# Expert tiles fixed per expert, overflow tiles between them, routing begun during attention, and results scattered by token

## The chip, the cores and the metric

The kernel runs on one core of a Trainium2 chip. Its engines are TensorE (matrix products; PE in the rows, and PEld for its weight loads), VectorE (DVE), ScalarE (ACT), GpSimd (POOL) and SyncE (SP), which here only issues DMAs. They run side by side and order themselves by semaphores. The metric is the time of one execution on the device in microseconds (us), lower is better.

## The reference

One layer of an encoder for 1024 tokens of width 1024, in float32. A first half (norm, one projection, a gated delta rule with 4 heads, a sliding window attention with 8 heads, an output projection) gives `x`; the change leaves its arithmetic alone. The second half is a mixture of experts:

```python
gl = tok @ w_group + b_group                     # 4 groups
p_top, g_idx = lax.top_k(jax.nn.softmax(gl), 1)  # the best group
el_sel = ...                                     # logits of the 4 experts in that group
e_val, e_idx = lax.top_k(el_sel, TOP_K)          # the best 2 of the 4
e_w = jax.nn.softmax(e_val, axis=-1) * p_top
...
for e in range(N_EXPERTS):                       # 16 experts, width 256
    gu = tok @ w_gate_up[e]
    act = jax.nn.silu(gu[:, :D_EXPERT]) * gu[:, D_EXPERT:]
    y = y + gates[:, e:e + 1] * (act @ w_down[e])
```

and the output is `x + y`. So there are 2048 picks, two for each token. With the inputs of these runs an expert gets 59 to 232 of them. In tiles of 128 rows that is 9 experts with one tile and 7 with two, 23 tiles.

## The kernel before

**Attention.** `run_tiles` runs over 8 tiles of 128 tokens, written out in full for each engine. A tile's `body` holds the delta rule and the attention; the projections of the next tile and the `late` part of the previous one (output projection, norm, router logits `lg`) are put between its steps. The last tile has no next tile, and its own `late` comes behind it alone. The normed rows go to `h_mid` in HBM and the residual to `x_mid`.

**Routing.** With all logits there, VectorE computes picks and gates for all 8 tiles at once (L1214 to L1237). TensorE sums the picks to ranks within each expert. From ranks and the number of tiles of each expert VectorE computes each pick's slot. One-hot rows (`hot_mod`, `hot_div`, L1268 and L1269) are multiplied on TensorE, which inverts the table: for each slot the token in it (`idx`, L1271).

**Experts.** The slots fill tiles in the order of the experts, an expert's second tile right behind its first, and there are always 31 of them (`SLOT_TILES`), the most that 2048 picks can need. `run_slots` writes the first three and last two steps out and has the rest in a loop. Per tile `m`: GpSimd gathers 128 rows of `h_mid` (L1426); TensorE turns them (L363), multiplies them with gate and up (64 passes of 128x128, L360) and the previous tile's result with `w_down`; VectorE copies the turned rows (L1278) and makes SwiGLU (L1285, L1287); VectorE and ScalarE copy half of the result each (L1294, L889); SP stores it to `y_slots`. TensorE's order in a step is: turn `m + 1`, gate/up `m`, down `m - 1`. Weights, gathered rows and results have two buffers each, and the weights' expert number is read from a table. If tile `m` isn't used (`m >= n_used`), its weights are not loaded and its gate/up and down are a stand-in of 4 columns; it is gathered, turned, copied and stored all the same.

**Combining.** When all tiles are stored, GpSimd gathers for each of 8 token tiles the two result rows of each token (L1434, L1436), VectorE scales them by the gates and adds them to `x` (L1310, L1314), and SP stores.

The whole of the expert stage's order on TensorE is this:

```python
def step(m, b, u):
    if not isinstance(m, int) or m < SLOT_TILES - 1:
        turn_rows(m + 1, 1 - b, u + b)
    gate_up(m, b, u)
    if later(m):
        down(m - 1, 1 - b, u - 1 + b)
```

## Time and profile before

| | us |
|---|---|
| median of 3 runs | 1135.8 |
| lowest and highest | 1134.96 and 1136.03 |
| the profiled execution | 1135.93 |
| its span, first to last instruction | 1134.2 |
| TensorE busy | 996.4 (88%) |
| VectorE busy | 569.7 (50%) |
| ScalarE busy | 237.8 (21%) |
| GpSimd busy | 116.4 (10%) |
| data moved by DMA | 155.38 MB |

The profile is of one execution, times in it are us from the start of the span, and what lies between span and time is 1.7 us. In the timeline a row has its start, its length, engine, line, operation, output and inputs, how many instructions are merged, and in square brackets how long the engine had been idle before it and who ended that. Float32 products go through TensorE in two passes, so a product counts as two there. An indirect DMA's row on GpSimd is the issue alone, not the transfer.

### The profile page before, as it was taken

What the parts mean: (1) busy time and instruction counts of PE and PEld (TensorE: products, weight loads), DVE (VectorE), ACT (ScalarE), POOL (GpSimd) and SP (SyncE); (2) the same over time, 40 slices, a digit from 0 to 9 for tenths busy, and PEclk for the clock granted to TensorE, in tenths of its full rate; (3) what the DMA queues carried; (4) which work ended last, traced back from release to release, by engine and by line L of the source; (5) the groups of instructions that cost most, each with busy time, mean ns of one, the idle gap of its engine ahead of it and who ended that gap; (6) DMA issues with size and microseconds to landing.
All of it is one profiled execution on the core that took longest, in us unless ns stands there. A gap on an engine that the chain in (4) does not pass through costs nothing.

```text
span 1134.2 us, 17951 instructions
## 1 busy us (share of the span) xinstructions
PE 996.4 (88%) x6940; PEld 693.9 (61%) x6940; DVE 569.7 (50%) x1654; ACT 237.8 (21%) x489; POOL 116.4 (10%) x182
## 2 busy tenths in 40 slices
PE   6979999999999999999999787643999999999820
PEld 2446656656656656656656556423888888888620
DVE  1455766765765756766756656345222121212445
ACT  1333233233233233233233221000000000000110
POOL 6020010010010010010010010000100000000124
PEclk9999999999999999999999978775899999999855
DMA  9700100100100100100000001045799999998668
GB/s 324 279 19 1 38 5 35 38 12 28 38 19 21 38 1 38 38 8 30 20 1 38 20 0 39 19 185 212 258 366 365 370 361 372 358 369 327 220 220 351
DMA packets 57312, 155.38 MB, mean 137 GB/s; under 512 B 4240, under 2 KB 5520, under 8 KB 57248
## 3 DMA queue, kind: packets, MB, share of 16 engines
q1 hardware_dynamic: 48752, 129.59, 30.9%
q0 software_dynamic: 6768, 24.64, 6.1%
q8 instruction: 44, 0.72, 0.3%
q10 hardware_dynamic: 1728, 0.26, 0.1%
q14 instruction: 20, 0.16, 0.0%
HBM read 125.65 MB, written 28.84 MB: 136 GB/s over the span
## 4 chain that ended last, share of the span: by engine, by line
PE 84%; DVE 7%; DMA 3%; issue 2%; POOL 2%; ACT 1%; SPq 0%; POOLq 0%; ACTq 0%; DVEq 0%
PE pm L360 77%; PE pm L363 8%; DMA w_sb<-h_mid,w_sb 1%; DMA w_sb<-y_slots,w_sb 1%; DVE X L1107 1%; DMA y_slots<-w_sb 1%; POOL w_sb L1436 1%; DVE w_sb L1200 1%; POOL w_sb L1434 1%; ACT ci L725 0%; DMA xt<-in_x 0%; DVE hT L935 0%; DVE bs L914 0%; DVE bs L913 0%; DVE bs L912 0%
## 5 line engine op out<-in xcount | busy, mean ns | idle before, releaser
L360 PE MATMUL pm<-w_sb,hT 128*128 128x512 f32 (+1 forms) x768 | 314.1, 564 | 2.9 <-DVE hT L935 2.8
L360 PE MATMUL pm<-w_sb 128*128 128x128 f32 (+2 forms) x1688 | 256.4, 314 | 8.6 <-DVE w_sb L1269 8.5
L360 PEld LDWEIGHTS pm<-w_sb,hT 128*128 128x128 f32 x768 | 144.2, 192 | 149.5 <-issue 141.2
L360 PEld LDWEIGHTS pm<-w_sb 128*128 128x128 f32 x1688 | 206.6, 196 | 42.0 <-issue 33.0
L360 PE MATMUL pm<-wo_sb,pT 128*128 128x512 f32 x256 | 120.5, 627 | 1.2 <-ACT pT L782 1.2
L1294 DVE COPY w_sb<-pm 128x512 f32<-128x512 f32 x31 | 21.4, 691 | 175.7 <-PE pm L360 168.3
L977 DVE SCALAR_TENSOR_TENSOR pqkv<-ci,cw,pqkv 128x128 f32<-128x128 f32 x288 | 77.6, 344 | 21.5 <-ACT pqkv L730 21.1
L360 PEld LDWEIGHTS pm<-wo_sb,pT 128*128 128x128 f32 x256 | 50.3, 201 | 60.4 <-issue 58.8
L1278 DVE TENSOR_TENSOR w_sb<-pm,gain 128x512 f32<-128x512 f32 x62 | 39.9, 685 | 40.4 <-PE pm L363 38.9
L1426 POOL DMA_INDIRECT w_sb<-h_mid,w_sb x31 | 29.2, 943 | 289.0 <-PE pm L363 262.7
L1107 DVE TENSOR_TENSOR X<-X,pm 128x256 f32<-128x256 f32 (+1 forms) x40 | 16.8, 419 | 80.2 <-PE pm L360 80.2
L881 ACT ACTIVATE w_sb<-pm 128x256 f32<-128x256 f32 x31 | 11.9, 383 | 213.0 <-PE pm L360 209.9
L1378 POOL TENSOR_TENSOR tail<-tail,rows 128x512 f32<-128x512 f32 x8 | 10.2, 1273 | 404.0 <-ACT aTm L749 404.0
L1023 DVE TENSOR_TENSOR sc<-sc,pm 128x512 f32<-128x512 f32 x16 | 11.0, 688 | 79.7 <-PE pm L360 79.7
L363 PE MATMUL pm<-ident,w_sb 128*128 128x128 f32 x248 | 37.7, 303 | 13.1 <-DMA w_sb<-h_mid,w_sb 11.2
L363 PEld LDWEIGHTS pm<-ident,w_sb 128*128 128x128 f32 x248 | 32.7, 157 | 26.1 <-issue 16.6
L363 PE MATMUL pm<-ident,y_mix 128*128 128x128 f32 x128 | 20.5, 312 | 22.9 <-DVE y_mix L1184 14.1
L889 ACT ACTIVATE w_sb<-pm 128x512 f32<-128x512 f32 x31 | 18.5, 597 | 84.2 <-PE pm L360 75.2
L818 ACT ACTIVATE Y<-pm 128x256 f32<-128x256 f32 (+1 forms) x48 | 18.3, 381 | 81.9 <-PE pm L360 81.9
L363 PEld LDWEIGHTS pm<-ident,y_mix 128*128 128x128 f32 x128 | 16.8, 159 | 27.8 <-DVE y_mix L1184 14.5
L719 ACT ACTIVATE tail<-pm 128x512 f32<-128x512 f32 (+1 forms) x24 | 12.7, 528 | 100.3 <-PE pm L360 100.3
L360 PEld LDWEIGHTS pm<-Y,aTm 64*64 64x64 f32 x576 | 22.1, 135 | 15.4 <-issue 11.8
(238 smaller groups left out, 1228.7 us busy)
## 6 DMA issues: line engine op xcount, KB each, us to landing
w_sb<-in_w_gate_up SPq DMA_DIRECT2D x23, 2048.0 KB
w_sb<-in_w_down SPq DMA_DIRECT2D x23, 1024.0 KB
y_slots<-w_sb SPq DMA_DIRECT2D x31, 512.0 KB
w_sb<-in_w_in SPq DMA_DIRECT2D x5, 2048.0 KB, 17.0
xt<-in_x SPq DMA_DIRECT2D x8, 512.0 KB, 3.5
wo_sb<-in_w_out SPq DMA_DIRECT2D x1, 4096.0 KB, 22.6
sc<-in_x SPq DMA_DIRECT2D x8, 512.0 KB, 3.5
x_mid<-sc SPq DMA_DIRECT2D x8, 512.0 KB, 2.6
```

The costliest lines, as they stand in the source:

```text
L360: return pe.matmul(o_, lhsT=l_, rhs=r_, start=start, stop=stop, skip_group_check=True)
L363: return pe.transpose(o_, in_, ident[:, :])
L719: act.activation(dst, pm[BANK[c]][:, 0:n], ACT.Copy).then_inc(F.chunk_copied, 1)
L818: act.activation(Yd[rows_], heads(pm[3], CH)[rows_], ACT.Copy).then_inc(B.y_copied, 1)
L881: act.activation(tnh, pm[2 + b][:, 0:DE], ACT.Tanh, scale=0.5).then_inc(M.tanh_ready, 1)
L889: act.activation(yo[b][:, 512:], pm[7][:, :], ACT.Copy).then_inc(M.y1_ready, 1)
L977: ins = v.scalar_tensor_tensor(cv[:, i, :], ci[:, i, j:j + P], cw[:, j, i:i + 1], cv[:, i, :], ALU.mult, ALU.add)
L1107: v.tensor_tensor(Xd[rows_], Xd[rows_], heads(pm[2], CH)[rows_], ALU.subtract).then_inc(B.x_updated, 1)
L1200: step(v.tensor_tensor(dst, a, b, op))
L1278: v.tensor_tensor(hgT[b][:, 4 * n:4 * n + 4, :], heads(pm[n]), wide(gain2[:, 4 * n:4 * n + 4]), ALU.mult).then_inc(M.hT_ready, 1)
L1294: v.tensor_copy(yo[b][:, 0:512], pm[6][:, :]).then_inc(M.y0_ready, 1)
L1426: g.indirect_dma_start(hg[m % 2], None, h_mid, bass.IndirectOffsetOnAxis(idx[:, m:m + 1], 0)).then_inc(gathered[m % 2], 16)
```

## The change

- There are again 31 steps, but 16 of them are fixed, one for each expert (`ORDER`, static), and 15 are overflow steps for ranks from 128 on (dynamic), which read their expert from a table. They alternate: S0, S1, D0, S2, D1, S3, ..., D13, S15, D14. With 7 experts over 128 picks, D0 to D6 are full and D7 to D14 are empty. Where the step is empty TensorE now skips the turn too. Row numbers that no token has are out of range, and the DMAs leave such rows out (`bounds_check`).
- All steps are written out. Fixed experts' weights have four buffers (three in the space of `w_in`, one in pieces of attention's tiles), the overflow steps one. The weights of experts 0 to 2 are loaded when the last tile's projections are done.
- The picks of tiles 0 to 5 are routed in the last tile's `body` (`picks_ahead`, `rank_ahead`) and `late` (`rows_ahead`); tiles 6 and 7 afterwards. The table is now by rank and expert, and there is a second one with the gates.
- The two halves of a result are scaled by the gate as they are copied, and GpSimd scatters them by pick to `y_picks`. The end is 16 plain loads, two sums for each tile and 8 stores.

VectorE in the last tile. Before (`upper` is the causal mask, `sc` the residual, `ctmp` and `Y` masks of the delta rule):

```order
L1080 TENSOR_TENSOR ctmp<-ctmp,upper 128x512 [waits dT_exp]
L1023 TENSOR_TENSOR sc<-sc,pm 128x512 [waits out_done,xr_loaded]
L1023 TENSOR_TENSOR sc<-sc,pm 128x512 [waits out_done]
L1084 TENSOR_TENSOR ctmp<-ctmp,bs 128x512
L1086 TENSOR_TENSOR Y<-pm,ctmp 64x4x64 [waits kk_done,back_step]
```

After, with 29 operations of `picks_ahead` in between:

```order
L1316 TENSOR_TENSOR ctmp<-ctmp,upper 128x512 [waits dT_exp]
L1063 TENSOR_REDUCE w_sb<-lg 128x6 [waits route_iotas,back_step]
L1050 TENSOR_TENSOR w_sb<-lg,w_sb 128x6x4 [waits route_route_step]
...
L1124 TENSOR_TENSOR w_sb<-w_sb 128x16 [waits route_route_step] x6
L1258 TENSOR_TENSOR sc<-sc,pm 128x512 [waits out_done,xr_loaded]
L1258 TENSOR_TENSOR sc<-sc,pm 128x512 [waits out_done]
L1322 TENSOR_TENSOR ctmp<-ctmp,bs 128x512
```

The first of them waits for GpSimd's iotas. GpSimd at the end of attention, before:

```order
L1405 TENSOR_TENSOR kn<-kn,bs 128x512 [waits kn_turned,eg_ready,kn_ready]
L1413 IOTA w_sb 128x128 [waits lg_ready]
L1414 CAST w_sb<-w_sb 128x128 [waits pool_made]
L1415 IOTA w_sb 128x8 [waits pool_made]
L1416 CAST w_sb<-w_sb 128x8 [waits pool_made]
```

GpSimd at the same place after the change, and on to the first gathers and scatters (L1651, L1659):

```order
L1628 TENSOR_TENSOR kn<-kn,bs 128x512 [waits kn_turned,eg_ready,kn_ready]
L1636 IOTA w_sb 128x128 [waits chunk_done]
...
L1645 MEMSET w_sb 128x16 [waits pool_made]
L1651 DMA qkvT<-h_mid,w_sb 128x1024 [waits route_rows_ready,mid_stored]
L1651 DMA pqkv<-h_mid,w_sb 128x1024
L1651 DMA qkvT<-h_mid,w_sb 128x1024 [waits slots_turned,route_spill_ready]
L1651 DMA pqkv<-h_mid,w_sb 128x1024 [waits slots_turned]
L1659 DMA y_picks<-tail,w_sb 2048x1024 [waits slots_y1_ready,slots_y0_ready]
L1651 DMA qkvT<-h_mid,w_sb 128x1024 [waits slots_turned]
```

The iotas no longer wait for the last logits, the third gather waits for the overflow rows, and from then on gathers and scatters take turns.

TensorE from the first tile on, before:

```order
L363 MATMUL pm<-ident,w_sb 128x128 x7
L360 MATMUL pm<-w_sb 128x128 [waits w1_loaded0,slots_hT_ready]
L360 MATMUL pm<-w_sb 128x128 x31
L363 MATMUL pm<-ident,w_sb 128x128 [waits slots_hT_ready,gathered0]
L363 MATMUL pm<-ident,w_sb 128x128 x7
L360 MATMUL pm<-w_sb 128x128 [waits w1_loaded1,slots_hT_ready]
```

After (`qkvT` and `pqkv` are now the buffers of gathered rows):

```order
L427 MATMUL pm<-ident,qkvT 128x128 [waits route_table_ready,gathered0]
L427 MATMUL pm<-ident,qkvT 128x128 x7
L427 MATMUL pm<-ident,pqkv 128x128 [waits slots_hT_ready,gathered1]
L427 MATMUL pm<-ident,pqkv 128x128 x7
L424 MATMUL pm<-ctmp,w_sb 128x128 [waits slots_hT_ready,w1_loaded0]
L424 MATMUL pm<-ctmp,w_sb 128x128 x31
L740 COMPARE_AND_BRANCH [waits slots_hT_ready,gathered0]
L427 MATMUL pm<-ident,qkvT 128x128 x8
L740 UNCONDITIONAL_BRANCH
L424 MATMUL pm<-ident 128x4
L742 UNCONDITIONAL_BRANCH
```

The order of turn, gate/up and down is as before; the third turn, an overflow tile's, stands behind a branch and before the second gate/up.

The diff, cut to its core:

```diff
-SLOT_TILES = (TOPK * T - NE) // P + NE
+RANKS = T // P
+SPILL = (TOPK * T - NE) // P
+RING = 4
+AHEAD = NT - 2
+
+ORDER = [(True, 0), (True, 1)]
+for _j in range(SPILL):
+    ORDER.append((False, _j))
+    if _j + 2 < NE:
+        ORDER.append((True, _j + 2))
+STEPS = len(ORDER)
...
+            def load_gate_up(e):
+                src = w_gate_up[0, e].rearrange("(k p) n -> p k n", p=P)
+                if e >= RING:
+                    sp.wait_ge(M.gu_done, AT[True, e - RING] + 1)
+                if e % RING < RING - 1:
+                    sp.dma_start(ring[e % RING][0], src).then_inc(w1_loaded[e % RING], 16)
+                    return
+                for i, dst in enumerate(apart_gu):
+                    sp.dma_start(dst.rearrange("p (k n) -> p k n", k=2),
+                                 src[:, 2 * i:2 * i + 2, :]).then_inc(w1_loaded[e % RING], 16)
...
+                if nx is None:
+                    sp.wait_ge(F.chunk_done, 6 * NT)
+                    for e in range(RING - 1):
+                        load_gate_up(e)
+                        load_down(e)
...
+            load_gate_up(RING - 1)
+            load_down(RING - 1)
+            sp.wait_ge(R.ready, 1)
...
+            load_dyn_gate_up(0)
+            load_dyn_down(0)
+            for p in range(STEPS):
+                next_gate_up(p)
+                if p:
+                    next_down(p - 1)
+            next_down(STEPS - 1)
...
+            for t in range(NT):
+                sp.dma_start(a_rows[t], y_picks[t * P:(t + 1) * P, :]).then_inc(ab_loaded[t // 2], 16)
...
+            def rank_ahead():
+
+                n = AHEAD * NE
+                pe.wait_ge(F.chunk_copied, 6 * NT)
+                pe.wait_ge(F.ci_copied, 3 * NT)
+                pe.wait_ge(A.picks, 1)
+                mm(pm[1][:, 0:n], upper_strict[:, :], picks[:, 0:n], True, False)
+                mm(pm[1][:, 0:n], ones[:, :], cums[:, 0:n], False, True).then_inc(A.ranked, 1)
+
+            def rows_ahead():
+                pe.wait_ge(F.hT_ready, 2 * NT)
+                for c in range(TOPK):
+                    for t in range(AHEAD):
+                        u = c * NT + t
+                        pe.wait_ge(A.hots, c * AHEAD + t + 1)
+                        mm(pm[0][:, 0:P], hot_mod[u], hot_row[u], u == 0, False)
+                        mm(pm[3][:, 0:P], hot_mod[u], hot_gate[u], u == 0, False)
+
...
+                if nx is None:
+                    rank_ahead()
...
+            def turn_rows(p):
+                static, i = ORDER[p]
+                pe.wait_ge(gathered[p % 2], 16 * (p // 2) + 16)
+                if p:
+                    pe.wait_ge(M.hT_ready, 2 * p)
+                else:
+                    pe.wait_ge(R.table_ready, 1)
+
+                def products():
+                    for k in range(KD):
+                        ins = turn(pm[k // 4][:, (k % 4) * P:(k % 4 + 1) * P], hg[p % 2][:, k * P:(k + 1) * P])
+                    ins.then_inc(M.turned, 1)
+
+                def nothing():
+                    mm(pm[0][:, 0:4], ident[:, :], ident[:, 0:4]).then_inc(M.turned, 1)
+
+                if_used(static, i, products, nothing)
...
+            turn_rows(0)
+            for p in range(STEPS):
+                if p + 1 < STEPS:
+                    turn_rows(p + 1)
+                gate_up(p)
+                if p:
+                    down(p - 1)
+            down(STEPS - 1)
...
+            def picks_ahead():
+
+                v.wait_ge(R.iotas, 1)
+                route_step(route_picks(0, AHEAD, A.exp_in))
+                all_picks = both_picks.rearrange("p t g e -> p t (g e)")
+                for t in range(AHEAD):
+                    ins = v.tensor_tensor(cum[:, t + 1, :], cum[:, t, :], all_picks[:, t, :], ALU.add)
+                    if t < AHEAD - 1:
+                        route_step(ins)
+                ins.then_inc(A.picks, 1)
+
+            def rows_ahead():
+
+                route_experts(0, AHEAD)
+                v.wait_ge(A.rank_ready, 1)
+                route_rows(0, AHEAD, rank)
+                v.wait_ge(A.exp_out, 1)
+                route_step(gates(0, AHEAD))
+                v.wait_ge(F.h_turned, NT)
+                v.wait_ge(F.chunk_done, 6 * NT)
+                for c in range(TOPK):
+                    for t in range(AHEAD):
+                        row_hots(c, t)
+                        gate_hot(c, t).then_inc(A.hots, 1)
+
+            def gates(t0, n):
+
...
+            def row_hots(c, t):
+
+                u = c * NT + t
+                v.tensor_scalar(hot_mod[u], iota_f, mod_of[:, c, t:t + 1], None, ALU.is_equal)
+                return v.tensor_scalar(hot_row[u], iota_f, comb_of[:, c, t:t + 1], row_f[:, c, t:t + 1], ALU.is_equal,
+                                       ALU.mult)
+
+            def gate_hot(c, t):
+                return v.tensor_scalar(hot_gate[c * NT + t], iota_f, comb_of[:, c, t:t + 1], gate_of[:, c, t:t + 1],
+                                       ALU.is_equal, ALU.mult)
...
+                if nx is None and nn is None and t == NT - 1:
+                    picks_ahead()
...
+            def spill_rows():
+
+                for j in range(0, SPILL, 4):
+                    n = min(4, SPILL - j)
+                    tt(sel_eq[:, 0:n, :], iota_f.unsqueeze(1).broadcast_to([P, n, P]), over_last(comb_f[:, j:j + n], P),
+                       ALU.is_equal)
+                    for src, dst in ((0, row_d), (1, gate_d)):
+                        tt(sel_in[:, 0:n, :], sel_eq[:, 0:n, :], table[:, src:src + 1, :].broadcast_to([P, n, P]), ALU.mult)
+                        step(v.tensor_reduce(dst[:, j:j + n], sel_in[:, 0:n, :], AX_X, ALU.add))
+                v.wait_ge(R.rows_ready, 1)
+                rows_of(row_d, SPILL, in_d, out_d).then_inc(R.spill_ready, 1)
+
...
+            copy_rows(0)
+            copy_rows(1)
+            spill_rows()
+            for p in range(STEPS):
+                if 0 < p < STEPS - 1:
+                    copy_rows(p + 1)
+                if p:
+                    copy_out(p - 1)
+                swiglu(p)
+            copy_out(STEPS - 1)
+
...
+                tt(x_rows[t], x_rows[t], a_rows[t], ALU.add)
+                v.tensor_tensor(x_rows[t], x_rows[t], b_rows[t], ALU.add).then_inc(M.summed, 1)
...
-            g.wait_ge(B.lg_ready, NT)
+            g.wait_ge(F.chunk_done, 6 * NT)
...
+            def gather(p):
+                static, i = ORDER[p]
+                if p > 1:
+                    g.wait_ge(M.turned, p - 1)
+                g.indirect_dma_start(hg[p % 2], None, h_mid,
+                                     bass.IndirectOffsetOnAxis((in_s if static else in_d)[:, i:i + 1], 0),
+                                     bounds_check=T - 1, oob_is_err=False).then_inc(gathered[p % 2], 16)
+
+            def scatter(p):
+                static, i = ORDER[p]
+                g.wait_ge(M.y0_ready, p + 1)
+                g.wait_ge(M.y1_ready, p + 1)
+                g.indirect_dma_start(y_picks, bass.IndirectOffsetOnAxis((out_s if static else out_d)[:, i:i + 1], 0),
+                                     yo[p % 2], None, bounds_check=TOPK * T - 1, oob_is_err=False).then_inc(y_stored[p % 2], 16)
 
...
+            g.wait_ge(R.rows_ready, 1)
+            gather(0)
+            gather(1)
+            g.wait_ge(R.spill_ready, 1)
+            gather(2)
+            for p in range(STEPS):
+                if p + 3 < STEPS:
+                    gather(p + 3)
+                scatter(p)
```

## Rows read from the trace of the kernel before

**Rows 1.** Stretches of time: columns as in the first line.

```profile
core 0: us, PE busy (x) PEld busy (x) DVE busy (x) ACT busy (x) POOL busy (x), PEclk, DMA share, GB/s
785.00:800.00 15.00, 7.00 (x32) 6.63 (x33) 2.58 (x4) 0.00 (x0) 2.88 (x4) 0.50 1.00 373
860.00:900.00 40.00, 40.00 (x271) 32.29 (x270) 10.91 (x20) 3.86 (x8) 3.75 (x4) 1.00 1.00 363
```

**Rows 2.** Timeline of one tile in the expert stage: start and length in us first.

```profile
840.19 1.04 PE L363 MATMUL pm<-ident,w_sb 128*128 128x128 f32 x8
...
848.41 0.38 ACT L881 ACTIVATE w_sb<-pm 128x256 f32<-128x256 f32 x1 [7.34 <-PE pm L360]
...
850.74 0.41 DVE L1285 SCALAR_TENSOR_TENSOR w_sb<-w_sb,pm 128x256 f32<-128x256 f32 x1
...
851.64 1.04 PE L363 MATMUL pm<-ident,w_sb 128*128 128x128 f32 x8
```

**Rows 3.** The page: costliest groups (POOL), then the DMA issues (SPq).

```profile
L1426 POOL DMA_INDIRECT w_sb<-h_mid,w_sb x31 | 29.2, 943 | 289.0 <-PE pm L363 262.7
...
w_sb<-in_w_gate_up SPq DMA_DIRECT2D x23, 2048.0 KB
```

**Rows 4.** Timeline, empty tiles and the first gather of the tail.

```profile
1058.72 0.28 PE L360 MATMUL pm<-ident 128*128 128x4 f32 x2
...
1066.38 0.94 POOL L1426 DMA_INDIRECT w_sb<-h_mid,w_sb  x1 [1.54 <-PE pm L363]
...
1069.04 1.97 PE L363 MATMUL pm<-ident,w_sb 128*128 128x128 f32 x8 [1.54 <-DMA w_sb<-h_mid,w_sb]
...
1092.32 0.60 ACT L889 ACTIVATE w_sb<-pm 128x512 f32<-128x512 f32 x1 [2.35 <-PE pm L360]
1095.88 0.94 POOL L1434 DMA_INDIRECT w_sb<-y_slots,w_sb  x1 [19.68 <-DMA y_slots<-w_sb]
```

**Rows 5.** Timeline from the end of the logits to the first tile.

```profile
758.07 0.19 DVE L1214 TENSOR_REDUCE w_sb<-lg 128x8 f32<-128x32 f32 x1 [1.68 <-POOL w_sb L1418]
...
765.67 0.29 DVE L1231 TENSOR_TENSOR w_sb<-w_sb 128x128 f32<-128x128 f32 x1
...
775.24 0.34 DVE L1268 TENSOR_SCALAR w_sb<-w_sb 128x128 f32<-128x128 f32 x1
775.50 0.23 DVE L1269 TENSOR_SCALAR w_sb<-w_sb 128x32 f32<-128x32 f32 x1
...
775.79 7.04 PE L360 MATMUL pm<-w_sb 128*128 128x32 f32 x32 [8.54 <-DVE w_sb L1269]
...
776.72 0.41 SPq L310 DMA_DIRECT2D w_sb<-in_w_gate_up  x1
...
783.92 1.15 POOL L1426 DMA_INDIRECT w_sb<-h_mid,w_sb  x1 [25.96 <-DVE w_sb L1271]
...
791.53 1.97 PE L363 MATMUL pm<-ident,w_sb 128*128 128x128 f32 x8 [8.71 <-DMA w_sb<-h_mid,w_sb]
...
796.71 9.28 PE L360 MATMUL pm<-w_sb 128*128 128x128 f32 x64
```

**Rows 6.** Timeline of VectorE and GpSimd in the last attention tile.

```profile
672.96 0.69 DVE L1023 TENSOR_TENSOR sc<-sc,pm 128x512 f32<-128x512 f32 x1 [3.71 <-PE pm L360]
...
673.44 1.04 POOL L1405 TENSOR_TENSOR kn<-kn,bs 128x512 f32<-128x512 f32 x1 [12.47 <-PE pm L363]
...
680.17 0.69 DVE L1023 TENSOR_TENSOR sc<-sc,pm 128x512 f32<-128x512 f32 x1 [6.52 <-PE pm L360]
```

**Rows 7.** Timeline, router products of tile 6, then the last `late`.

```profile
692.25 1.86 PE L360 MATMUL pm<-w_rt,pT 128*128 128x20 f32 x16
...
737.57 0.69 DVE L1023 TENSOR_TENSOR sc<-sc,pm 128x512 f32<-128x512 f32 x1 [12.60 <-PE pm L360]
...
749.39 1.79 PE L363 MATMUL pm<-ident,y_mix 128*128 128x128 f32 x8 [5.06 <-DVE y_mix L1029]
...
752.57 3.60 PE L360 MATMUL pm<-w_rt,pT 128*128 128x20 f32 x16 [1.38 <-DVE pT L1035]
```

**Rows 8.** Timeline of VectorE, a sum over 128x512 in SBUF.

```profile
720.46 0.69 DVE L1181 TENSOR_REDUCE bs<-Y 128x4 f32<-128x512 f32 x1
```

More of the change, by code:

```diff
@@ L50 @@
 TOPK = 2
-SLOT_TILES = (TOPK * T - NE) // P + NE
+RANKS = T // P
[8 more added lines that the diff above has]
+STEPS = len(ORDER)
+AT = {tile: _p for _p, tile in enumerate(ORDER)}
 LEVELS = [2, 4, 8, 16, 32, 64]
@@ L177, in build @@
+        none, shift, to_f = part(NE), part(NE), part(NE)
+        in_s, out_s, in_d, out_d = [part(NE).bitcast(I32) for _ in range(4)]
         y_mix = sb("y_mix", [D])
@@ new lines, in _ @@
+            route_picks(AHEAD, NT - AHEAD, R.exp_in).then_inc(R.picks, 1)
+            v.wait_ge(R.picks, 1)
+            route_experts(AHEAD, NT - AHEAD)
+            v.wait_ge(R.counts, 1)
+            route_rows(AHEAD, NT - AHEAD, pm[1][:, 0:(NT - AHEAD) * NE].rearrange("p (t e) -> p t e", e=NE))
+            for c in range(TOPK):
+                for t in range(AHEAD, NT):
+                    ins = row_hots(c, t)
+            ins.then_inc(R.hots, 1)
+            v.wait_ge(R.exp_out, 1)
+            step(gates(AHEAD, NT - AHEAD))
@@ new lines, in _ @@
+            v.wait_ge(R.rows_summed, 1)
+            step(v.tensor_copy(table[:, 0, :], pm[0][:, 0:P]))
+            rows_of(table[:, 0, 0:NE], NE, in_s, out_s).then_inc(R.rows_ready, 1)
+            for c in range(TOPK):
+                for t in range(AHEAD, NT):
+                    ins = gate_hot(c, t)
+            ins.then_inc(R.gate_hots, 1)
+            v.wait_ge(R.totals, 1)
+            tt(over, over_last(pm[2][:, 0:NE], RANKS), steps_f.unsqueeze(1).broadcast_to([P, NE, RANKS]),
+               ALU.is_gt)
@@ L1430, in _ @@
[L1430 to L1437 removed]
+            step(g.tensor_copy(iota_e, iota_f[:, 0:NE]))
```

554 lines of the change are left out of this document (294 added, 260 removed).

## The prediction

> **What bounds the kernel now.** I read the table of stretches first [rows 1]. The attention part runs until about 750 us, and the change touches only its last tile. Behind it, at 785 to 800 us, TensorE is busy for less than half of the time and its clock is granted at 0.50 (its level of 1.2 GHz). In the expert stage, of which 860 to 900 us stands for all from 820 to 1040, TensorE is busy for all 40 us at a granted clock of 1.00 (2.4 GHz), and the DMA engines are at 1.00 of their time as well. From about 1060 us to the end nothing useful is multiplied any more [rows 4].
>
> The timeline gives the durations. In the expert stage the turning of rows for one tile starts at 840.19 and the next at 851.64, so a tile costs 11.46 us and TensorE has no idle time in front of it [rows 2]: this stage is bound by TensorE, with the DMA just keeping up. 23 tiles have whole weight loads; 31 are gathered and stored [rows 3]. So 8 of the 31 are empty. They run from 1058.7 us (the first 128x4 stand-in) to 1092.9 us, 34.2 us or 4.3 us each, on a chain through gather, VectorE, ScalarE and the store [rows 4]. The tail runs from 1095.9 us to the end at 1134.2, 38.3 us [rows 4].
>
> The routing chain starts when the last logits are copied (1.68 us before 758.07: 756.4, called L). The first gather starts at 783.92, and the first turn at 791.53, L + 35.1 [rows 5]. From 791.53 the 23 tiles would take 263.5 us; the first runs partly at the half clock (its gate/up takes 9.28 us [rows 5]), and work that counts ends 4 us behind the first stand-in, near 1062.7 [rows 4].
>
> **The change part by part.**
>
> *Last attention tile.* VectorE gets 29 small routing operations (23 and 6 sums) between the product with `upper` and the two sums into `sc`. Before, 35 such operations took from 758.07 to 765.96, 0.226 us each [rows 5]; at 6 tiles instead of 8 I take 0.22, so 6.3 us. VectorE is idle there from 669.25 to 672.96 and from 673.65 to 680.17 [rows 6], 10.2 us, which would hide them. But they wait for the iotas, and these now stand on GpSimd behind `kn<-kn,bs`, which ends at 674.48 [rows 6]. Ten small GpSimd operations follow; six took most of the 1.68 us that VectorE waited for them [rows 5], ten take 2.4. The routing thus starts at 676.9 and ends at 683.2, and the two sums behind it (0.65 us apart) end at 684.6 instead of 680.8. All that is queued behind on VectorE, the masks that TensorE waits for next among it, is **3.9 us** late. If the wait did not bite this is 0; if the rest of the tile adds idle TensorE and half clock, 6.
>
> *Rows ahead, before the last output projection.* 4 + 10 + 4 small operations (about 4.0 us by 0.226) and 36 one-hot rows. From a 128 wide one to the next operation it was 0.26 us [rows 5], so 36 x 0.26 = 9.4: 13.4 us, against 12.60 us in which VectorE waits for the first half of the projection [rows 7]. Hidden. On TensorE 24 products of 128x128 come behind the projection: two passes each at 0.113 us (the 64 passes of gate/up lie between 841.1 and 848.4 [rows 2]), 5.4 us, against 5.06 us in which TensorE waits for `hm` [rows 7]: +0.3. In exchange TensorE stays busy, and the router product that took 3.60 us at half clock should take the 1.86 us of the tile before [rows 7]: -1.7. Net **-1.4** (from -3 to +3). So L becomes 756.4 + 3.9 - 1.4 = 758.9.
>
> *Routing behind L.* 23 operations on two tiles at 0.195 (the spacing of the narrow ones): 4.5 us. Products on TensorE at half clock, three in a row, leave a wait: 1.6 with the 4 operations under it. 10 operations 2.0; 8 one-hots 2.1; then TensorE's four products at the half clock's 0.44 us each (32 passes in 7.04 us, two per product [rows 5]) 1.8 and semaphores 0.3; copy and 5 operations 1.2. The first gather can start at L + 13.5, not L + 27.5. It has no weight loads beside it, since three experts' weights come during attention; a gather beside tiny loads took 2.66 us from start to the turn it released [rows 4]. But the first turn also waits for the gate table: 4 one-hots 1.0 and about 18 operations, three of them 240 wide, 4.5: L + 19.0 = **777.9** against 791.5.
>
> *The third gather.* Here the gain is partly given back. The third step is an overflow tile, and its gather waits for the overflow rows, which VectorE computes after the first two tiles are copied: 20 operations of 128x512 or 128x384 (0.69 us for such a sum in SBUF [rows 8]; 0.73 with the gap, 0.59 for the last five): 13.9, and 1.0 for five more. The two copies in front end 6.7 us after the first turn starts (the second turn ended at 796.7 [rows 5], and its copy is two operations of 128x512). So gather 2 starts at 777.9 + 6.7 + 14.9 + 0.2 = 799.7 and lands at 802.4. TensorE's order is turn 0, turn 1, gate/up 0, turn 2: it is done with gate/up 0 at 792.4 (14.5 us after its start, as from 791.53 to 806.0 before [rows 5]) and stands 10 us. The clock falls to its half as in 785 to 791 before [rows 1].
>
> *The 23 tiles.* At 802.4 TensorE has done 9.1 of its 263.5 us (two turns at 0.9, gate/up 7.3); 254.4 remain, plus 3 for the clock's rise (gate/up took 9.28 from 796.71 instead of 7.3, and a turn 1.97 instead of 1.04 [rows 2, 5]). I leave 11.46 per tile: TensorE sets it. DMA moves less (rows that carry no token are out of range, 2048 rows instead of 31 x 128), weights are four experts ahead, and the one buffer pair for overflow tiles has 16 us between release and need against some 8.6 us of load (2 MB and 1 MB at 363 GB/s [rows 1]).
>
> *Eight skipped steps*, seven of them between fixed tiles. TensorE's own share is three stand-ins (0.28 us for two passes [rows 4]), some 0.6 us. And the chain now shows: after gate/up of tile S the skipped tile's copy (0.69 for 128x512 [rows 7]) stands before the two SwiGLU operations (0.41 each [rows 2]), so `down` starts 2.1 us after gate/up ends, where before a `down` of 3.4 us covered this; 1.5 us of it is new idle time after the stand-ins and the next turn are taken off. With a gather that arrives now and then late I take 2.3 each, **16** for seven; from 1.2 (no wait but the chain) to 4.3 (the old rate [rows 4]). End of TensorE: 802.4 + 254.4 + 3 + 16 + 0.7 = 1076.5.
>
> *Tail.* Copy, last scatter and landing: 4.5 us, 1081. Then 16 plain loads of 512 KB and 8 stores, 12.6 MB as before; 38.3 us becomes 35, since x comes in beside the last tiles, the issue by SP replaces 16 gathers. Bounds: 34 (12.6 MB at the 373 GB/s of [rows 1]) and 39. End 1116; with the 1.7 us that lie between span (1134.2) and time (1135.93) **1118 us**. The profiled run is the median of the runs to 0.1 us, so nothing is scaled.
>
> **Where the skill weighs in.** Gather 0 landed 7.6 us after its start although some 6 MB of weights had been issued from 776.72 on [rows 5]; at 373 GB/s [rows 1] those alone would have lasted until about 794. The row leaves open whether a gather waits its turn behind the weights. The Trainium skill, DMA: Bandwidth & Descriptors, section Queues, rings and completion order, says each DMA engine takes turns between the queues that have work, packet by packet. By that rule a gather isn't held behind a 2 MB load and the skipped steps keep near 2.3 us; without it the first rival below holds. The Trainium skill, DMA: Bandwidth & Descriptors, section Anatomy of one DMA, puts most of a DMA's fixed cost of about 2 us on the confirmation of the last write; by it a gather in which every row is out of range would save data time only, and the 2.66 us above would be about 2.9 instead; no row here shows one.
>
> **The rivals.**
>
> *A, slower: GpSimd's queue sets the skipped steps.* A gather now stands behind a scatter, which waits for the output of its step. After gate/up of a fixed tile ends at T, the skipped tile's scatter starts at T + 1.3 and the next gather at T + 2.5; TensorE wants it at T + 5.6. The next fixed tile's gather starts at T + 7.6 and is wanted at T + 13.6. If both land 7.6 us after their start, as gather 0 did under weights [rows 5], the first is 4.5 late and the second, with 6.0 of slack, 1.6. With the 1.8 of the chain that makes 7.9 us per step instead of 2.3: 7 x 5.6 = 39, 1157 us. It decides from 4.8 us a step, where the 1135.8 of before is reached. Against it: in this phase DMA needs 3.7 MB per 13 us, 280 GB/s of 363 and more [rows 1].
>
> *B, better: the covers hold.* The iotas' wait is taken up by slack (-3.9) and a skipped step costs 1.2 (-8): 1106.
>
> *C: empty still costs.* If an out-of-range row is still moved or written as a descriptor, or branches in the unrolled code starve TensorE's sequencer, the skipped steps cost 3.8 and the tail 38: +11 +3, 1132. For it: the old empty steps cost 4.3 with every row moved [rows 4].
>
> **How the numbers follow.** Forecast (1112 to 1125) 50%, A 10%, B 20%, C (1125 to 1134) 20%. What a measurement here tells from no change is 0.2%, 2.3 us. Faster needs below 1133.5: all of the forecast and B, most of C and a tenth of A: 0.85. Same 0.05, slower 0.10. The range for 8 in 10: A's far end (10%) and the best part of B (8%) are left out: 1104 to 1136.
>
> **What would show it.** Right: the sums into `sc` of the last tile near 684 us and picks before them starting right when GpSimd's iotas end; first turn of rows near 778; a TensorE gap of about 10 us before the third turn, ended by a gather behind VectorE's 128x512 products; fixed tiles 11.46 us apart while overflow tiles are full, and 13 to 14 us per pair of fixed and skipped one afterwards; last scatter near 1078. Wrong: gaps of 4 us and more ended by gathers in the second half (A), no gap before the third turn, or full tiles that are not 11.46 us.

## The result, and the profile after

| | us |
|---|---|
| the kernel before, median of 4 | 1135.7 |
| the changed kernel, median of 4 (1146.6 to 1158.9) | 1149.8 |
| ratio after to before, of the means | 1.0138, 95% interval 1.0076 to 1.0199 |
| profiled execution after, its span | 1152.15, 1150.0 |
| forecast (range) | 1118 (1104 to 1136) |

The change made the kernel 1.4% slower. I had forecast 1.6% faster, with 10% for slower: wrong, in sign and beyond the range.

The stretches first, against [rows 1]:

```profile
core 0: us, PE busy (x) PEld busy (x) DVE busy (x) ACT busy (x) POOL busy (x), PEclk, DMA share, GB/s
785.00:800.00 15.00, 8.93 (x66) 8.74 (x64) 13.95 (x22) 0.00 (x0) 0.00 (x0) 0.84 1.04 399
860.00:900.00 40.00, 37.72 (x266) 31.10 (x265) 8.36 (x15) 3.34 (x7) 6.10 (x6) 1.00 0.93 328
1000.00:1040.00 40.00, 30.88 (x178) 26.23 (x178) 10.97 (x20) 4.21 (x8) 8.13 (x8) 0.83 0.55 193
```

At 860 to 900 us TensorE used to be busy for all 40 us; now it lacks 2.3 of them although the DMA engines have less to do (0.93 for 1.00). At 1000 to 1040 us, where each second step is skipped, it stands for 9 of 40 us with the DMA at 0.55, and its granted clock has fallen to 0.83. Neither TensorE nor the DMA engines are at their limit, so something waits for something else to be issued. The profile's chain of work that ended last names it (with shares of the span):

```profile
PE pm L424 69%; PE pm L427 6%; DMA pqkv<-h_mid,w_sb 5%; DMA qkvT<-h_mid,w_sb 2%; DMA wo_sb<-y_picks 1%; DMA y_picks<-tail,w_sb 1%; DVE X L1345 1%; POOL y_picks L1659 1%; DVE w_sb L1050 1%; DVE S L1050 0%; DVE w_sb L1493 0%; ACT ci L845 0%; 
```

7% of the span, some 80 us, hangs on the gathers (`<-h_mid`); before it was 1%. The chain counts a gather from its issue on; TensorE's idle time in front of late turns is less, 11.2 us at the third turn, 6.6 in the full steps and 13.8 in the skipped ones. The timeline of one full overflow step and one fixed step, against [rows 2] (TensorE's turns and GpSimd's issues alone):

```profile
843.05 1.09 PE L427 MATMUL pm<-ident,pqkv 128*128 128x128 f32 x8 [0.84 <-DMA pqkv<-h_mid,w_sb]
843.80 1.01 POOL L1659 DMA_INDIRECT y_picks<-tail,w_sb  x1 [9.94 <-ACT tail L1009]
845.12 1.02 POOL L1651 DMA_INDIRECT qkvT<-h_mid,w_sb  x1 [0.30 <-issue]
854.57 1.04 PE L427 MATMUL pm<-ident,qkvT 128*128 128x128 f32 x8
856.32 1.00 POOL L1659 DMA_INDIRECT y_picks<-w_sb  x1 [10.18 <-PE pm L427]
857.63 1.02 POOL L1651 DMA_INDIRECT pqkv<-h_mid,w_sb  x1 [0.30 <-issue]
867.61 1.09 PE L427 MATMUL pm<-ident,pqkv 128*128 128x128 f32 x8 [1.42 <-DMA pqkv<-h_mid,w_sb]
```

The buffer `pqkv` is read out at 844.1, but its next gather starts at 857.63: GpSimd takes the scatter first, and that one waits until the step's result is copied (10.18 us idle). TensorE wants the rows 8.6 us after that issue, at 866.19, and gets them after 10.0, at 867.61; from 830 to 960 us such a gather takes 9.8 us to land (median for `pqkv`). Before, nothing stood in between:

```profile
841.50 0.94 POOL L1426 DMA_INDIRECT w_sb<-h_mid,w_sb  x1 [10.52 <-PE pm L363]
```

This is the kernel before: the gather starts 0.3 us behind the turn of 840.19 and has 21.6 us until the turn that needs it (863.10). The same place in a pair with a skipped step, after the change (SPq are the weight loads of the next fixed expert, 2 MB and 1 MB):

```profile
1001.79 0.38 SPq L313 DMA_DIRECT2D w_sb<-in_w_gate_up  x1
...
1003.69 1.01 POOL L1659 DMA_INDIRECT y_picks<-tail,w_sb  x1 [9.16 <-PE pm L427]
...
1005.01 1.02 POOL L1651 DMA_INDIRECT qkvT<-h_mid,w_sb  x1 [0.30 <-issue]
...
1007.30 0.40 SPq L324 DMA_DIRECT2D w_sb<-in_w_down  x1
...
1011.34 0.59 PE L424 MATMUL pm<-ident 128*128 128x4 f32 x2 [4.07 <-DMA qkvT<-h_mid,w_sb]
1011.78 9.83 PE L424 MATMUL pm<-ci,w_sb 128*128 128x128 f32 x64
```

The gather of an empty tile moves no row, yet it lands 6.0 us after its issue. TensorE wanted it 2.3 us after that issue and waits 4.07 us for it, and the gate/up behind runs at a lower clock (9.83 us; it is 7.39 where nothing waited). Once no weights are in flight such a gather lands in 2.1 us (median); 2.4 us after its issue TensorE is at its stand-in, and nobody waits:

```profile
1063.53 1.02 POOL L1651 DMA_INDIRECT qkvT<-h_mid,w_sb  x1 [0.30 <-issue]
...
1065.95 0.38 PE L424 MATMUL pm<-ident 128*128 128x4 f32 x2 [0.16 <-issue]
```

The front, against [rows 5]: picks, router product, and the first and third turn.

```profile
678.17 0.18 DVE L1063 TENSOR_REDUCE w_sb<-lg 128x6 f32<-128x24 f32 x1 [7.67 <-POOL w_sb L1645]
...
756.55 2.77 PE L424 MATMUL pm<-w_rt,pT 128*128 128x20 f32 x16 [1.38 <-DVE pT L1270]
...
779.12 1.94 PE L427 MATMUL pm<-ident,qkvT 128*128 128x128 f32 x8 [2.71 <-DVE w_sb L1483]
...
805.10 1.96 PE L427 MATMUL pm<-ident,qkvT 128*128 128x128 f32 x8 [11.17 <-DMA qkvT<-h_mid,w_sb]
```

And the end, against [rows 4]: eight loads of `x_mid`, the last scatters, and the copy that waits for the scatter two steps ahead of it.

```profile
1101.16 3.75 SPq L409 DMA_DIRECT2D w_sb<-x_mid  x8
...
1102.24 0.99 POOL L1659 DMA_INDIRECT y_picks<-tail,w_sb  x1 [7.25 <-ACT tail L1009]
...
1109.34 0.75 DVE L1521 TENSOR_SCALAR tail<-pm,w_sb 128x512 f32<-128x512 f32 x1 [3.66 <-DMA y_picks<-tail,w_sb]
...
1110.87 0.98 POOL L1659 DMA_INDIRECT y_picks<-tail,w_sb  x1 [2.51 <-DVE tail L1521]
...
1116.51 0.32 SPq L413 DMA_DIRECT2D w_sb<-y_picks  x1
```

The forecast's span was 1116.3, the span is 1150.0. The 33.7 us between them lie here:

| stretch | forecast | after | more |
|---|---|---|---|
| to the third turn | 802.4 | 805.1 | 2.7 |
| third turn to first skipped turn, 14 steps | 163.4 | 170.0 | 6.6 |
| the seven skipped steps between fixed tiles, each | 2.3 | 5.3 | 21.3 |
| last skipped turn to TensorE's end | 14.4 | 14.0 | -0.4 |
| TensorE's end to last row stored | 4.5 | 9.8 | 5.3 |
| tail | 35.3 | 33.5 | -1.8 |

The skipped steps' turns run from 975.11 to 1092.68: 117.6 us for seven pairs, 16.8 each, less 11.46. TensorE ends at 1106.7; the expectations below counted from 0.8 us earlier and say 10.6 for 9.8.

### The profile page after: what moved, and what is told of

The parts are those of the page before. It is cut to its first block, busy times and chain, and to the rows that moved or that the text cites. A ratio compares the mean times of both kernels' runs of the same rounds, so it can differ in the third digit from the quotient of the medians.

```text
span 1150.0 us, 17416 instructions
## 1 busy us (share of the span) xinstructions
PE 1001.1 (87%) x6936; PEld 695.3 (60%) x6936; DVE 596.3 (52%) x1736; ACT 240.7 (21%) x491; POOL 130.5 (11%) x201
## 4 chain that ended last, share of the span: by engine, by line
PE 75%; DMA 10%; DVE 8%; issue 3%; ACT 2%; POOL 1%; SPq 1%; POOLq 0%; ACTq 0%; DVEq 0%
PE pm L424 69%; PE pm L427 6%; DMA pqkv<-h_mid,w_sb 5%; DMA qkvT<-h_mid,w_sb 2%; DMA wo_sb<-y_picks 1%; DMA y_picks<-tail,w_sb 1%; DVE X L1345 1%; POOL y_picks L1659 1%; DVE w_sb L1050 1%; DVE S L1050 0%; DVE w_sb L1493 0%; ACT ci L845 0%; SPq L413 0%; DMA xt<-in_x 0%; ACT tail L1009 0%
## 5 line engine op out<-in xcount | busy, mean ns | idle before, releaser
L424 PE MATMUL pm<-ci,w_sb 128*128 128x128 f32 x704 | 87.3, 289 | 0.0
L424 PEld LDWEIGHTS pm<-ci,w_sb 128*128 128x128 f32 x704 | 86.1, 205 | 0.0
L1521 DVE TENSOR_SCALAR tail<-pm,w_sb 128x512 f32<-128x512 f32 x16 | 12.0, 750 | 116.0 <-PE pm L424 112.3
L1345 DVE TENSOR_TENSOR X<-X,pm 128x256 f32<-128x256 f32 (+1 forms) x40 | 16.8, 419 | 81.2 <-PE pm L424 81.2
L424 PE MATMUL pm<-ctmp,wo_sb 128*128 128x128 f32 x448 | 51.2, 275 | 0.0
L424 PEld LDWEIGHTS pm<-ctmp,wo_sb 128*128 128x128 f32 x448 | 50.6, 192 | 0.0
L424 PE MATMUL pm<-w_sb,Y 128*128 128x512 f32 x96 | 43.6, 597 | 2.2 <-DVE Y L1513 2.2
L427 PE MATMUL pm<-ident,pqkv 128*128 128x128 f32 x216 | 30.8, 284 | 10.9 <-DMA pqkv<-h_mid,w_sb 8.3
L1503 DVE TENSOR_TENSOR ctmp<-pm,gain 128x512 f32<-128x512 f32 x32 | 20.6, 686 | 33.0 <-PE pm L424 19.3
L427 PEld LDWEIGHTS pm<-ident,pqkv 128*128 128x128 f32 x216 | 24.6, 146 | 19.9 <-DMA pqkv<-h_mid,w_sb 13.4
L427 PE MATMUL pm<-ident,y_mix 128*128 128x128 f32 x128 | 19.7, 304 | 17.4 <-DVE y_mix L1422 14.2
L424 PE MATMUL pm<-aTm,Y 64*64 64x64 f32 (+1 forms) x656 | 34.9, 230 | 0.0
```

What stands on the lines that cost most here:

```text
L424: return pe.matmul(o_, lhsT=l_, rhs=r_, start=start, stop=stop, skip_group_check=True)
L427: return pe.transpose(o_, in_, ident[:, :])
L1345: v.tensor_tensor(Xd[rows_], Xd[rows_], heads(pm[2], CH)[rows_], ALU.subtract).then_inc(B.x_updated, 1)
L1503: v.tensor_tensor(hgT[b][:, 4 * n:4 * n + 4, :], heads(pm[n]), wide(gain2[:, 4 * n:4 * n + 4]), ALU.mult).then_inc(M.hT_ready, 1)
L1521: v.tensor_scalar(yo[b][:, 0:512], pm[4 + 2 * b][:, :], slot_gate(p), None, ALU.mult).then_inc(M.y0_ready, 1)
```

## The experiments

Each is an edit of the changed kernel. Where its ratio to the kernel before is given, it is of runs on the same chip; differences to the changed kernel are of medians (1149.8). Its four runs spread over 12 us, and the medians of the kernel before differ by 1.4 us from chip to chip (1135.7 to 1137.1), so a difference of less than some 7 us is not clear from the times alone; there the traces have to carry it.

### Gathers ahead of scatters

```diff
             gather(2)
+            gather(3)
             for p in range(STEPS):
-                if p + 3 < STEPS:
-                    gather(p + 3)
+                if p + 4 < STEPS:
+                    gather(p + 4)
                 scatter(p)
```

> Theory 1 (order on GpSimd): in the changed kernel the gather of step p+3 stands behind the scatter of step p-1, so it is issued at 857.63 although its buffer was read out at 844; it then has 10 us before its turn, and lands 0.6 to 1.7 us late in the full steps and up to 4.2 us late in the skipped ones. Here the gather of step p+4 stands ahead of the scatter of step p, so each gather is issued one step earlier. Expected: no turn of rows waits for a DMA, a pair of a full and a skipped step takes 13.3 us as the last two of the changed kernel (not 17.4 to 20.0), a full step 11.46; the ratio to the changed kernel 0.975, about 1122 us. Theory 2 (the data path): gathers land late because weights are in flight, whenever they are issued; then a gather issued earlier only waits longer in the queue, at most a third of the 28 us comes back: 1140 to 1150. Theory 3 (the chain of a skipped step, matmul and copies and semaphores, is itself 6 us long): the full steps gain 6 us, the pairs stay: 1143.

Measured 1122.6, ratio to before 0.9874 (0.9847 to 0.9901): 27.2 us less than the changed kernel. Timeline of the second half (TensorE's turns of skipped and fixed tiles, GpSimd's gathers):

```profile
1002.91 1.02 POOL L1651 DMA_INDIRECT qkvT<-h_mid,w_sb  x1 [0.30 <-issue]
...
1007.58 1.07 PE L427 MATMUL pm<-ident,pqkv 128*128 128x128 f32 x8
...
1012.72 0.28 PE L424 MATMUL pm<-ident 128*128 128x4 f32 x2
...
1020.46 1.07 PE L427 MATMUL pm<-ident,pqkv 128*128 128x128 f32 x8
```

and its stretches:

```profile
860.00:900.00 40.00, 40.00 (x290) 33.88 (x289) 8.36 (x15) 3.55 (x7) 7.10 (x7) 1.00 0.99 345
...
980.00:1020.00 40.00, 39.11 (x267) 31.77 (x266) 16.54 (x30) 5.97 (x11) 12.15 (x12) 1.00 0.86 295
```

From the fourth on no turn waits, TensorE is busy for 40 of 40 us at 860 to 900, and a pair takes 12.88 us, all but the first (15.3), in which `down` of the last full tile stands. The seven pairs take 92.6 us for 117.6; of these 25.0 us 13.8 are the waits themselves. The DMA engines are busier than in the changed kernel (0.99 for 0.93 at 860 to 900, and 0.86 for 0.62 at 980 to 1020), so theory 2 falls. Nor do the gathers land sooner: from 990 to 1060 us the median from issue to landing is 5.4 and 6.2 us for the two buffers, against 5.8 and 5.5 in the changed kernel. They are only issued a step earlier. Theory 3 falls too: a skipped step costs 1.4 us (12.88 less 11.46), where it costs 5.2 in the changed kernel, both without the first pair. That also answers the prediction's rival C: the branches and the descriptors of empty tiles don't cost 3.8 us a step.

### The weights of experts 12 to 15 left out

```diff
+                if e >= 12:   # one row in place of the matrix, for w_gate_up and w_down
+                    sp.dma_start(ring[e % RING][0][0:1, 0, :], src[0:1, 0, :]).then_inc(w1_loaded[e % RING], 16)
+                    return
```

> The weights of the fixed experts 12 to 15 are left out (one row of each is loaded instead, so their products are of old numbers); all else is the changed kernel. In the changed kernel the four pairs of a full and a skipped step in which these 12 MB are loaded take 17.4 to 20.0 us, and the pairs behind them, with no weights in flight, 13.3; the gather of an empty tile takes 6.3 us from issue to landing beside the weights and 2.4 us without. Theory 1+2 (a gather that is issued late AND is stretched by the weights): all pairs take 13.3 to 13.8, 18 to 21 us less than the changed kernel: about 1129. If weights in flight have no part in it (the gather's time is its own, only the order sets it): the first pairs stay at 17 to 20 us, and the time within 3 us of the changed kernel. If the price were in the clock alone (stalls first, clock after), the stalls must come first, so it reads as the first case.

Measured 1134.8, 15.0 less and not the 18 to 21 expected. Its profiled run had reached the first turn 4.1 us later than that of the changed kernel, so the stage itself gained more: the seven pairs took 96.2 us (979.79 to 1075.97) for 117.6. The gathers of empty tiles, now in 2.1 us (median of the even buffer), were in time:

```profile
1006.97 1.02 POOL L1661 DMA_INDIRECT qkvT<-h_mid,w_sb  x1 [0.30 <-issue]
1009.38 0.39 PE L434 MATMUL pm<-ident 128*128 128x4 f32 x2
```

The full steps ahead, with their weights in flight, still wait 0.6 to 1.9 us each. So the 4 us waits need both: a gather issued late, and a transfer that weights stretch.

### Both together

> Both edits of the first call: gathers ahead of scatters by one step, and the weights of the fixed experts 12 to 15 left out (one row of each is loaded). The weights alone were worth 15 us and the order alone 27 us. If both act through the same wait (a gather issued late and stretched by weights), the sum is not 42 but 27: with the gathers issued early the weights cost nothing, and this runs within 2 us of the kernel with early gathers (1122.5), that is 1121 to 1124. If weights in flight also slow something else (TensorE's operands, the scatters, the last copies), it comes out well below: 1108 to 1117.

Measured 1124.0, within 1.5 us of the early gathers alone. With the gathers issued early these 12 MB of weights cost nothing, so they acted through this wait, and what followed from it, and through nothing else that the time shows.

### Idle products in the wait

```diff
+                if not static and 8 <= i <= 10:    # then: 9 <= i <= 11, four products
+                    pe.wait_ge(M.hT_ready, 2 * p)
+                    for k in range(8):
+                        mm(pm[0][:, :], ident[:, :], flat((ctmp, ci)[(p - 1) % 2])[:, 0:512])
                 pe.wait_ge(gathered[p % 2], 16 * (p // 2) + 16)
```

> The changed kernel, with eight idle products of 128x512 (3.6 us at full clock, results not used) on TensorE ahead of the wait for the gathered rows of overflow tiles 8, 9 and 10. These are the three turns that wait 4 us for their gather; behind that wait the next gate/up took 9.0 to 9.8 us at the lower clock instead of 7.4. Theory: each late gather costs twice, its 4 us of wait and about 2.9 us of lower clock behind it (pair of 20.0 = 12.9 + 4.2 + 2.9); here the wait stays but the clock holds, so the gate/up behind it takes 7.4 to 7.6 and the time is 6 to 9 us less: 1141 to 1144. Rival: the late gather alone makes the pairs long (then the idle products change nothing, or add what they outlast the wait by): 1149 to 1152.

A miss: 1156.4, 6.7 us more. I had taken 3.6 us for eight such products, the time of `down`'s eight passes, which are four products. Eight took 7.03 and outlasted the wait. What they did to the clock was as expected: the gate/up behind took 7.39. With four of them:

> The eight idle products took 7.0 us and not 3.6 and so outlasted the wait that they stood in; the clock did hold (gate/up 7.39 behind them). Here four of them (3.5 us) stand ahead of the wait for the gather of overflow tiles 9, 10 and 11, which waited 4.07, 4.17 and 3.69 us. Theory (a late gather costs its wait and then the lower clock, 2.4 us in the gate/up and the rest in the products behind it): the pairs come to 16.7 to 17.2 us instead of 18.4 to 20.0, and the time to 1141 to 1144. Rival: the clock price is not separate, the pairs stay within 0.5 us: 1149.

```profile
1009.52 7.39 PE L424 MATMUL pm<-ci,w_sb 128*128 128x128 f32 x64
...
1022.26 3.60 PE L424 MATMUL pm<-ci,ident 128*128 128x512 f32 x8
1026.59 0.39 PE L424 MATMUL pm<-ident 128*128 128x4 f32 x2 [0.73 <-DMA qkvT<-h_mid,w_sb]
```

Measured 1145.0 (1141.4 to 1149.8), 4.8 less, just above the range expected, and the times of the two kernels overlap; the trace carries this one. There the pairs that end at overflow tiles 10, 11 and 12 take 17.3, 16.7 and 13.3 us, where the changed kernel has 20.0, 19.7 and 14.9: 7.3 less with the gathers as late as ever (3.60 us of idle products and 0.6 to 0.7 of wait where 4.1 to 4.2 of wait were, in two of the three). So a wait of 4 us costs up to 3 us again behind it, through the clock. A shorter one need not: in the full steps of the changed kernel waits of 0.6 to 1.7 us were followed by gate/ups of 7.31 us.

### Three fixed tiles ahead of the first overflow tile

```diff
-ORDER = [(True, 0), (True, 1)]
+ORDER = [(True, 0), (True, 1), (True, 2)]
...
-            g.wait_ge(R.spill_ready, 1)
             gather(2)
+            g.wait_ge(R.spill_ready, 1)
```

> Three fixed tiles run before the first overflow tile (not two), and the third gather does not wait for the overflow tiles' rows. Theory (my step d): the 11.2 us for which TensorE waits ahead of the third turn of rows go, since gather and turn of fixed tile 2 need only the fixed rows; the fourth gather is then issued at 802 for a turn at about 808, and lands in time or up to 3 us late. Expected 8 to 11 us less than the changed kernel: about 1140. Rival: the wait moves to the fourth turn (VectorE still has 14 us of overflow rows to work out ahead of the first gated product): less than 3 us gained.

Measured 1141.7, 8.1 less (8 to 11 expected). The third turn starts at 793.04 with no wait; the fourth waits 3.23 us for its gather:

```profile
793.04 1.04 PE L427 MATMUL pm<-ident,qkvT 128*128 128x128 f32 x8
...
808.91 1.96 PE L427 MATMUL pm<-ident,pqkv 128*128 128x128 f32 x8 [3.23 <-DMA pqkv<-h_mid,w_sb]
```

### The iotas ahead of the last decay wait

The block of ten GpSimd instructions moves from behind the last `body` to ahead of its wait for `kn_ready`.

> The ten GpSimd instructions that make the iotas (2.4 us) stand ahead of the wait for the decay of kn of the last attention tile, in the 13.8 us that GpSimd idles there, not behind it. Theory: the picks on VectorE start when VectorE is free at 670.5 and not at 678.2, and the scores' copies behind them at 681 to 682: 3.7 us less at the end of attention and in the total (about 1146). Rival: the picks are not what sets the end of the last tile, the router's own chain is; then nothing changes (within 1 us).

Measured 1149.4, which is no gain by the median. In the trace the picks start at 671.81 and don't wait, and from the first copy of the tile (L1306) to the router product it is 87.3 us for 91.2: 3.9 less (3.7 expected). Of that the profiled execution keeps 2.5 at its end (a span of 1147.5 for 1150.0). That the median hides it is no wonder: the changed kernel's own four runs spread over 12 us. How much the mend is worth at the end stays open. Profiled executions of kernels without it, alike up to there, reach the router product between 755.7 and 761.5, at a granted clock of 0.67 to 0.80 in 690 to 720 us (752.0 to 754.1, at 0.83 to 0.86, in the four with the early iotas).

### The three mends together, and the end

> The three mends together: gathers ahead of scatters, three fixed tiles ahead of the first overflow tile with the third gather ahead of the wait for the overflow rows, iotas ahead of the last decay wait. Alone they gave 27, 8 and (in the trace, up to the router's product) 3.9 us, though of the last only 0.4 us stood in the median. Theory: the three waits lie one behind the other on the path, so the gains add: 1149.8 - 27.2 - 8.1 - 3.9 = 1110.6 (1108 to 1114), 2.3% below the kernel before. Rival: the wait for the overflow rows returns at the fourth turn as the early gathers make the steps ahead of it no shorter, and the gain of the order is all there is: 1118 to 1122.

Measured 1114.1 (ratio 0.981, 0.9794 to 0.9826), 3.5 short of the sum. TensorE ends at 1065.2, 12.9 us ahead of the kernel with early gathers, which looks like the 8.1 and 3.9 in full. But the split doesn't bear that out: 8.2 of the 12.9 are there at the router product already (752.35 against 760.60), where the iotas account for 3.9 and the rest is not explained; behind it the new order is 9.1 ahead at the fourth turn and gives 4.5 back, part of it by a gate/up of 9.37 us behind the 3.14 us wait of that turn. At the end, two empty tiles are now last, and one of their copies waits for a scatter beside the loads of `x_mid`:

```profile
1062.87 4.56 SPq L409 DMA_DIRECT2D w_sb<-x_mid  x8
1062.97 0.98 POOL L1663 DMA_INDIRECT y_picks<-tail,w_sb  x1 [4.14 <-DVE w_sb L1521]
...
1070.46 0.75 DVE L1521 TENSOR_SCALAR tail<-pm,w_sb 128x512 f32<-128x512 f32 x1 [6.75 <-DMA y_picks<-tail,w_sb]
...
1077.39 0.32 SPq L413 DMA_DIRECT2D w_sb<-y_picks  x1
```

12.1 us pass from TensorE's end to the last row stored, 3.0 more than with early gathers alone. First try at it: a fixed tile last, two pairs of overflow tiles side by side, and the eight loads at the start of overflow tile 13, still on SP.

> As the kernel with the three mends, with the end changed: fixed tile 15 is the last step (overflow tiles 9 and 10, and 13 and 14, stand side by side ahead of it), and the eight loads of x_mid are issued at the start of the step of overflow tile 13 and not behind the last step's loads. In the changed kernel the last copies wait 3.7 us for the scatter two steps earlier, which shares the queues with these 4 MB, and from TensorE's end to the last row stored it takes 10.6 us where I forecast 4.5. Theory: this comes down to 5 or 6, and the time by 4 to 6 us from the kernel with the three mends: 1105 to 1107. Rival: the two places with two skipped steps in a row cost what the end gains, since each skipped step's small load is issued behind the product of the one ahead and takes 2 us or more: 1110 to 1114.

A miss: 1122.8. The rival's place was right, its price too low:

```profile
1048.32 4.02 SPq L408 DMA_DIRECT2D w_sb<-x_mid  x8
...
1053.32 0.29 SPq L372 DMA_DIRECT2D wo_sb<-in_w_gate_up  x1
...
1063.21 1.51 PE L427 MATMUL pm<-ident 128*128 128x4 f32 x6 [9.37 <-DMA wo_sb<-in_w_gate_up]
```

The 2 KB load of the next overflow tile was issued at 1053.32 on the queue that had just been given 4 MB, and TensorE, which wanted it 0.5 us later, got it after 9.9. The other double, with a fixed expert's 3 MB of weights issued around its small load and no `x_mid`, cost 2.70 us of wait. No run has a double with nothing beside it, so what the place alone costs isn't shown. Second try: the order of the three mends, without doubles but for the last two tiles, the eight loads on ScalarE's queue at the start of fixed tile 14.

```diff
+                if p == AT[True, NE - 2]:
+                    act.wait_ge(L.mid_stored, 32 * NT)
+                    act.wait_ge(M.down_done, 2 * AT[True, NE - 3] + 2)
+                    for t in range(NT):
+                        act.dma_start(x_rows[t], x_mid[t * P:(t + 1) * P, :]).then_inc(L.x_loaded, 16)
                 act.wait_ge(M.gu_done, p + 1)
```

> The kernel with the three mends, with the eight loads of x_mid (4 MB) issued on ScalarE's queue at the start of the step of fixed tile 14, two fixed steps earlier, so that they are in before the last scatters. In the kernel with the three mends the last copies wait 7.4 us for the scatter of the overflow tile two steps earlier, which is under way beside these loads, and from TensorE's end to the last row stored it takes 12 us. Theory: the scatters at the end land in 3 to 4 us, the last row is stored 4 us earlier: 1109 to 1111. Rival: an all-skipped scatter takes its 5 to 7 us whatever is beside it: within 1 us of 1114; or the 4 MB then hold up the last weights or gathers: above 1115.

Measured **1106.8** (1104.2 to 1107.8), ratio to before 0.9735 (0.9713 to 0.9757): the best version, 2.6% below before and 43 us below the changed kernel. That is 7.3 less than with the three mends, where 3 to 5 were expected.

```profile
1062.94 0.97 POOL L1665 DMA_INDIRECT y_picks<-tail,w_sb  x1 [4.15 <-DVE w_sb L1523]
...
1066.25 0.75 DVE L1523 TENSOR_SCALAR tail<-pm,w_sb 128x512 f32<-128x512 f32 x1 [2.63 <-DMA y_picks<-tail,w_sb]
...
1067.78 0.97 POOL L1665 DMA_INDIRECT y_picks<-tail,w_sb  x1 [2.58 <-DVE tail L1523]
...
1069.87 0.36 SPq L410 DMA_DIRECT2D w_sb<-y_picks  x1
```

The copy can start 3.3 us after the scatter's issue and not 7.5, and it is 5.0 us from TensorE's end (1064.9) to the last row stored, where it was 12.1; that is nearly the whole gain.

## Why the prediction was wrong

- *Last attention tile, rows ahead, routing behind L*: right. The picks wait for the iotas, and the delta rule's masks behind them start at 685.77 instead of 680.78. Of these 5.0 us 1.2 are there at the tile's first copy (665.33 for 664.09), so the picks cost 3.8 (3.9 forecast); in the trace with the early iotas 4.0 go. L is 759.5 (758.9), the first turn 779.1 (777.9). That L agrees to 0.6 us is in part luck: profiled executions of the same code differ by 5.8 us there, and the router product took 2.77 us and not the 1.86 I had put.
- *The third gather*: right, 11.2 us of wait (10), though the turn starts at 805.1 and not 802.4. It was the part given back that I had seen, and moving the tile gives back 8.1 us of it.
- *The 23 tiles*: **wrong in "I leave 11.46 per tile: TensorE sets it"**. I checked the weights and the bandwidth there, and not the gathers' start. The gather of a fixed tile has 8.6 us from issue to need and takes 9.8 to land beside weights: 14 steps take 170.0 us, and 162.0 with the gathers issued early. The row that I had, `10.52 <-PE pm L363` in front of each gather (in [rows 3] as 262.7 of 289.0 us), shows that before it was released by the turn alone. The order of GpSimd's instructions, shown ahead of the prediction, has the scatter in between.
- *Eight skipped steps*: **the step that failed**. I wrote "with a gather that arrives now and then late I take 2.3 each"; it is 5.3, which is past the 4.8 from which rival A decides; that is 21.3 of the 33.7 us. Without the wait it is 1.8 on the same count (92.6 us for seven pairs), 1.4 without the first pair, so the chain itself was rated too high. Rival A named this mechanism and its place (a gather behind a scatter, landing too late), and had 10%. What I held against it was a rate (280 GB/s of 363), and the experiments show that rate isn't what decides: the kernel with early gathers moves more and doesn't wait. What decides is the time from issue to need, 2.3 us at 1005.01, against a landing of 6.0 us. A's sum came out at 1157 by other terms than the trace has: it took 7.6 us for every landing, let the fixed tile's gather be 1.6 us late as well, which no such gather between skipped steps was, and had no term for the clock.
- The rule that I weighed (the Trainium skill, DMA: Bandwidth & Descriptors, section Queues, rings and completion order: engines take turns between queues, packet by packet) is not borne out for empty gathers: the one issued at 1005.01 lands after 6.0 us, at 1011.0, and the 2 MB issued 3.2 us ahead of it after 9.4, at 1011.2. In all four late pairs the empty gather lands within 0.3 us of the fixed expert's 2 MB issued ahead of it (in the fourth, of the last of their four pieces). Whether it took turns with that load or was held behind it, these rows don't settle; either way I had read "not held behind" as "not slowed". The section Anatomy of one DMA of the same page gives a DMA a fixed cost of about 2 us, whatever its size; the trace agrees for a gather without rows with nothing beside it (2.1 us), and disagrees beside weights, where it shows 3.2 to 6.1 us in the four late pairs. The 2.9 us that I put there in place of the 2.66 follow from nothing shown; the row says 2.66.
- *Tail*: the loads take 33.5 us (35), but "copy, last scatter and landing: 4.5 us" was 9.8. I had priced the last scatter and not the wait of the last copy for the one two steps earlier, beside 4 MB of `x_mid`. With these loads moved it is 5.0. Rival C's term for this part, 38 us of tail, did not come.

With the queue's order mended and nothing else, the kernel takes 1122.6, 4.6 from the forecast: the sum was of a kernel in which gathers are issued when their buffer is free. That it is so near is in part luck. Against the forecast its profiled execution is 7.2 us late at the third turn and loses 4.6 between TensorE's end and the last row stored, and it is 1.4 ahead in the 14 full steps, 3.7 in the seven pairs and 1.7 in the rest.

## What to carry to other kernels

When a change puts a second kind of DMA on an engine's queue, write down for each transfer when its buffer is free, when its issue comes up behind the waits ahead of it, and when it is needed; issue prefetches ahead of stores that wait for results. Judge the lead against a transfer's time beside the traffic of that stage, not against bandwidth. And a wait on TensorE can cost more than its length, by what the clock loses behind it: here up to 3 us behind a wait of 4.
